# Layer norms from shifted sums taken beside the last projection, first and last recurrence pair beside projections, rotation without TensorE

## The chip, the cores and the metric

One NeuronCore of one Trainium2 chip runs the kernel. The metric is the device time of one execution in microseconds, the median of several runs. Engines are called by their profile names: PE (TensorE), DVE (VectorE), ACT (ScalarE), POOL (GpSimd), SP (SyncE, which here only issues DMAs).

## The reference

`reference()` takes x of 512 positions x 2048 channels through two blocks. Cut to what matters here:

```
first_block:  h = rms_norm(x)*(1+scale)+shift;  proj = h @ w_in
              q = rope(rms_norm(q)), k = rope(rms_norm(k)), 8 heads: sparse attention
              8 heads: chunked HGRN2 recurrence;  x += gate * (concat @ w_out)
second_block: y = even_layer(x)      # stick-breaking attention, pooling, @ w_out
              x = layer_norm(ALPHA * x + y, ln_g[0], ln_b[0])
              y = odd_layer(x)       # mixes x with its predecessor, @ w1, @ a1,
                                     # r,k,v,g = mixed @ w_r, w_k, w_v, w_g
                                     # wkv7 recurrence over 32 heads, group norm, @ w_o
              x = layer_norm(ALPHA * x + y, ln_g[1], ln_b[1])
layer_norm:   mean = mean(x); var = mean((x - mean)**2); (x - mean)*rsqrt(var+eps)*g + b
rope:         (t1*cos - t2*sin, t2*cos + t1*sin) of the two halves of a head's channels
```

All of it is float32.

## The kernel before

Activations lie transposed: 16 tiles `X[kt]` of 128 channels x 512 positions. Every projection is cut into groups `G` of 512 output channels; a group is four slots `k`, a slot covers four input tiles. SP loads a slot's weights (1 MB) into `RAW[k % 2]`, ACT copies them as rounded floats into `WH` (L308), DVE writes the remainder into `WL` (L313), and PE does three matmuls of 128x512 for each of the 16 pairs of input and output tile (`pe_slot`, L288 to L290): 192 matmuls a group. The result lies in four PSUM banks, `PJ` or `AB`. The input side is split in the same way when the source changes ("refill" number `e`: `act_refill` writes `XH`, L383, `dve_refill` writes `XL`, L388, tile by tile). Before the first slot of a refilled group PE waits for four `XL` tiles.

`act_group` and `dve_group` give the order on ACT and DVE: in step k >= 1 the split of the slot after next, then the side work `steps(k)`; after the last slot the evacuation `evac()`, side work 3 and 4, and the split of slot 1 of the next group. So side work placed in step k delays the next split on that engine.

The stages in order: modulation rows (`ada`), index keys and queries, selection of keys by DVE, eight attention heads (`att_*`; head h-1 is computed as side work of the projection group of head h), eight HGRN heads, the output projection `G_OUT1`, eight stick-breaking heads, four pooling groups, `G_OUT2` with its layer norm (`ln_pe`, `ln_act`, `ln_dve`, l = 0), the narrow group `G_LORA`, sixteen groups `G_RW` (r, k, v, g; stored to `rkvg_scratch` by POOL), the recurrence, `G_OUT3`, and the second layer norm.

In attention, the rotation of q and k is: PE multiplies both with a matrix that swaps the halves (L428), DVE forms AB * SIN and wk * COS and adds them (L490 to L493).

A layer norm here follows the evacuation of the last group: PE sums over the channels with a matrix of 1/2048 (L914), DVE subtracts the mean from 16 tiles (L936), ACT squares (L924), PE sums the squares (L917), ACT takes the root (L926), DVE the reciprocal (L939) and 16 products (L942), ACT scales and shifts (L929). After the first norm ACT and DVE then split the 16 tiles for the group `G_LORA`, whose slot 2 is split by DVE only after its first mixing step (L1123).

The recurrence is written as a loop over t from -3 (unrolled) in which each engine's list `wv_pe`, `wv_act`, `wv_dve`, `wv_sp`, `wv_pool` treats four pairs of heads at different stages. A pair's triangular block goes from SBUF to HBM (`sp_blocks_out`, L1241) and back (L1245), POOL solves it (L1291, L1294), the result goes out and back (L1259, L1264), DVE transposes it (L1649). Before the loop SP waits for all stores of r, k, v, g and for three memsets of POOL, writes zeros (L1790) and loads pairs 0 and 1. After it, ACT waits for all 16 pairs before the first split and refill of `G_OUT3`.

## Time and profile before

| what | us |
|---|---|
| median of 3 runs (3834.82 to 3844.33) | 3836.2 |
| the profiled execution | 3836.17 |
| its span in the trace | 3834.5 |
| PE busy in the span | 3507.2 (91%) |
| DVE busy | 1774.2 (46%) |
| ACT busy | 1399.7 (37%) |
| POOL busy | 364.6 (10%) |
| granted PE clock, mean | 0.955 of full |

Busy time of PE is the time in which any matmul was in flight. Times inside the trace count from the span's start. A matmul of a projection starts 0.23 us after the one before it although its own row says 0.4 us, because matmuls are pipelined. A "chain" is followed back from the last instruction of a window to what released each step, so it shows which engine set the end there.

### The profile page before, as it was taken

The numbers are of one execution on the slowest core, as the hardware profiler recorded it, in microseconds if no ns is written. First come the engines' busy times: TensorE is split into PE (matmuls) and PEld (weight loads), VectorE is DVE, ScalarE is ACT, GpSimd is POOL, SyncE is SP. The second block draws the span as 40 slices with busy tenths as digits, with TensorE's granted clock in tenths as the row PEclk, the third lists the DMA queues.
The fourth block names the chain that finished last, engine by engine and source line by source line (L and its number), as shares of the span: only waits on it lengthen the run. The fifth ranks groups of instructions, "written<-read, shape, count | busy, mean of one in ns | idle before, by whom it ended". The sixth has DMA issues, their size and how long they took to land.

```text
span 3834.5 us, 51471 instructions
## 1 busy us (share of the span) xinstructions
PE 3507.2 (91%) x21068; PEld 2729.5 (71%) x21068; DVE 1774.2 (46%) x2242; ACT 1399.7 (37%) x1625; POOL 364.6 (10%) x718
## 2 busy tenths in 40 slices
PE   8998899999998798999999987999999958888797
PEld 1476677777877587777777774888888846666584
DVE  3547645556666423333332336342424226776434
ACT  1322233243343212333322215241414137887323
POOL 0001121222121000000000000000000013333000
PEclk9998999999999799999999998999999979999798
DMA  8422122322222142222222222333333323332321
GB/s 303 174 77 74 66 96 90 98 99 87 90 94 85 61 161 103 77 77 77 88 90 85 99 89 81 119 118 114 120 120 131 109 68 76 73 78 59 107 96 66
DMA packets 178951, 381.37 MB, mean 99 GB/s; under 512 B 111728, under 2 KB 117104, under 8 KB 145008
## 3 DMA queue, kind: packets, MB, share of 16 engines
q1 hardware_dynamic: 164352, 326.73, 25.3%
q0 software_dynamic: 14448, 52.50, 4.1%
q8 instruction: 110, 1.80, 0.2%
q14 instruction: 41, 0.34, 0.0%
HBM read 342.49 MB, written 35.13 MB: 98 GB/s over the span
## 4 chain that ended last, share of the span: by engine, by line
PE 76%; DVE 9%; ACT 5%; DMA 3%; issue 3%; POOLq 2%; SPq 1%; DVEq 1%; ACTq 1%; POOL 0%
PE PJ L288 15%; PE PJ L290 15%; PE PJ L289 15%; PE AB L288 6%; PE AB L289 6%; PE AB L290 6%; PE AB L229 2%; DVE WL L313 1%; POOLq L1293 1%; POOLq L1290 1%; PE AB L917 1%; DVE XL L388 1%; DVE WK L853 1%; DMA WS<-solved_scratch 1%; DMA X<-blocks_scratch 1%
## 5 line engine op out<-in xcount | busy, mean ns | idle before, releaser
L288 PE MATMUL PJ<-XH,WH 128*128 128x512 f32 x2848 | 1138.6, 400 | 100.0 <-DVE XL L388 58.1
L290 PE MATMUL PJ<-XH,WL 128*128 128x512 f32 x2848 | 1119.1, 393 | 0.0
L289 PE MATMUL PJ<-XL,WH 128*128 128x512 f32 x2848 | 1118.9, 393 | 0.0
L313 DVE TENSOR_TENSOR WL<-RAW,WH 128x2048 fp32r<-128x2048 f32 (+2 forms) x240 | 552.9, 2305 | 729.7 <-ACT WH L308 724.7
L308 ACT ACTIVATE WH<-RAW 128x2048 fp32r<-128x2048 f32 (+2 forms) x240 | 453.0, 1889 | 917.1 <-PE PJ L290 633.8
L288 PEld LDWEIGHTS PJ<-XH,WH 128*128 128x128 f32 x2848 | 542.0, 190 | 224.7 <-issue 81.5
L289 PEld LDWEIGHTS PJ<-XL,WH 128*128 128x128 f32 x2848 | 542.1, 190 | 115.6 <-issue 5.0
L290 PEld LDWEIGHTS PJ<-XH,WL 128*128 128x128 f32 x2848 | 540.8, 190 | 115.1
L288 PE MATMUL AB<-XH,WH 128*128 128x512 f32 (+1 forms) x960 | 375.5, 391 | 25.3 <-DVE XL L388 22.4
L289 PE MATMUL AB<-XL,WH 128*128 128x512 f32 (+1 forms) x960 | 375.3, 391 | 0.0
L290 PE MATMUL AB<-XH,WL 128*128 128x512 f32 (+1 forms) x960 | 375.1, 391 | 0.0
L288 PEld LDWEIGHTS AB<-XH,WH 128*128 128x128 f32 (+1 forms) x960 | 179.3, 187 | 66.4 <-issue 26.6
L290 PEld LDWEIGHTS AB<-XH,WL 128*128 128x128 f32 (+1 forms) x960 | 179.3, 187 | 40.0
L289 PEld LDWEIGHTS AB<-XL,WH 128*128 128x128 f32 (+1 forms) x960 | 179.3, 187 | 39.7
L229 PE MATMUL AB<-WK,SMALL 128*1 128x512 f32 x192 | 90.8, 619 | 16.9 <-DMA WK<-ada 16.9
L1291 POOL TENSOR_TENSOR X<-X 128x30 f32<-128x30 f32 (+10 forms) x240 | 73.3, 305 | 218.0 <-DMA X<-blocks_scratch 185.6
L400 ACT ACTIVATE WK<-PJ 128x1024 f32<-128x1024 f32 (+1 forms) x23 | 23.1, 1005 | 178.8 <-PE PJ L290 178.8
L406 DVE COPY WK<-PJ 128x1024 f32<-128x1024 f32 (+1 forms) x31 | 37.4, 1207 | 101.7 <-PE PJ L290 101.6
L1856 POOL DMA_DIRECT2D rkvg_scratch<-WK x16 | 12.0, 753 | 741.7 <-DVE WK L1149 741.7
L540 POOL TENSOR_TENSOR TBL<-GATE,SMALL 128x512 f32<-128x512 f32 x16 | 16.8, 1048 | 660.0 <-PE AB L555 657.2
L1294 POOL TENSOR_TENSOR X<-X 128x30 f32<-128x30 f32 (+10 forms) x240 | 72.9, 304 | 34.7 <-issue 1.2
L229 PEld LDWEIGHTS AB<-WK,SMALL 128*1 128x1 f32 x192 | 15.1, 85 | 82.3 <-issue 82.2
(374 smaller groups left out, 3907.4 us busy)
## 6 DMA issues: line engine op xcount, KB each, us to landing
RAW<-w SPq DMA_DIRECT2D x232, 1024.0 KB, 4.8
WK<-ada SPq DMA_DIRECT2D x32, 1024.0 KB, 4.9
GATE<-gate POOLq DMA_DIRECT2D x64, 256.0 KB, 2.9
rkvg_scratch<-WK POOLq DMA_DIRECT2D x16, 1024.0 KB, 4.8
x_scratch<-X POOLq DMA_DIRECT2D x8, 1024.0 KB, 5.7
X<-rkvg_scratch SPq DMA_DIRECT2D x32, 256.0 KB, 3.4
RAW<-rkvg_scratch SPq DMA_DIRECT2D x32, 256.0 KB, 3.6
X<-xT SPq DMA_DIRECT2D x4, 1024.0 KB, 15.6
```

Of the source, the lines that this page charges most:

```text
L229: m = nc.tensor.matmul(AB[0:1, 2 + b, :], SILU[:, SKT * k + j:SKT * k + j + 1], WK[:, at:at + SEQ], start=k == 0 and j == 0, stop=False)
L288: nc.tensor.matmul(bank[0:width, n, :], hi, xh, start=first, stop=False)
L289: nc.tensor.matmul(bank[0:width, n, :], hi, xl, start=False, stop=False)
L290: m = nc.tensor.matmul(bank[0:width, n, :], lo, xh, start=False, stop=last)
L308: nc.scalar.activation(WH[k % 2][:, :, 0:w], narrow(RAW[k % 2], w), ACT.Copy).then_inc(wh_ready, 1)
L313: nc.vector.tensor_tensor(WL[k % 2][:, :, 0:w], narrow(RAW[k % 2], w), WH[k % 2][:, :, 0:w].bitcast(F32), ALU.subtract).then_inc(wl_ready, 1)
L388: nc.vector.tensor_tensor(tile(XL, kt), src(kt), tile(XH, kt).bitcast(F32), ALU.subtract).then_inc(xl_ready, 1)
L853: nc.vector.reciprocal(wk(12), wk(12))
L917: nc.tensor.matmul(AB[:, 1, :], mat("mean2048"), SQR[kt % 2], start=kt == 0, stop=kt == KT - 1).then_inc(s("ln_used"), 1)
L1290: nc.gpsimd.drain()
L1291: P_TT(SCRATCH[:, 0:c, 0:w], n[:, j:j + 1, j + 1:].to_broadcast([P, c, w]), SOLVED[:, 0:c, j:j + 1].to_broadcast([P, c, w]), ALU.mult)
L1294: m = P_TT(SOLVED[:, 0:c, j + 1:], SOLVED[:, 0:c, j + 1:], SCRATCH[:, 0:c, 0:w], ALU.subtract)
```

## The change

Six things are done.

- **Refilled groups.** `pe_slot` takes the input tile as its outer loop in a refilled group and waits for one `XL` tile at a time.
- **Rotation.** PE no longer swaps the halves. DVE reads the other half of the partitions directly: four instructions on 128x1024 or 64x1024 elements, all from SBUF.
- **Layer norms.** DVE has always summed the tiles as they were evacuated; now the sum of the first 12 tiles gives a provisional mean `SHIFT` after slot 0 of the last group. In steps 1 and 2 of that group DVE subtracts it from 12 tiles, ACT squares them, and POOL adds up the squares (11 additions). Tiles 12 to 15 are finished one by one in slot 3, between PE's output tiles, and PE sums them and their squares by eight small matmuls, among the group's own and behind them. The rest of the mean (`OFF`) is then subtracted by DVE (4 tiles) and POOL (12 tiles), the variance corrected by its square, and DVE's products begin. For l = 0 ACT writes `XH` directly from the product, and DVE's `XL` is interleaved with the products.
- **First pair.** Loads, decay, key norm and the first factor of pair 0 are computed as side work of the last `G_RW` group; SP loads both first pairs there, and POOL fetches the row of resets long before.
- **Last pair.** ACT and DVE split slot 0 and the finished tiles of `G_OUT3` while pair 15 is still worked on; PE waits only for what it needs.
- **Buffers.** Several buffers of the recurrence move so that the above do not overwrite each other (`ws`, `kept`, `T_*`); the lists of the loop keep their order.

```diff
+    wait(pe, wl_ready, g + 1)
+    order = [(n, j) for n in range(tiles) for j in range(SKT)]
     if refill is not None:
-        wait(pe, xl_ready, KT * refill + SKT * (k + 1))
...
+        order.sort(key=lambda nj: nj[1])
+    for n, j in order:
+        kt = SKT * k + j
+        if refill is not None and n == 0:
...
+        if between is not None and j == SKT - 1 and n < tiles - 1:
+            m.then_inc(s("ln_tile"), 1)
+            between(n)
...
-        wait(pe, s("at_qn"), h + 1)
-        for j in range(2):
-            m = nc.tensor.matmul(AB[:, j, :], mat("swap128"), wk(j), start=True, stop=True)
-        m.then_inc(s("at_swapped"), 1)
+        return
...
-        wait(dve, s("at_swapped"), h + 1)
-        for j in range(2):
-            nc.vector.tensor_tensor(wk(6 + j), AB[:, j, :], SIN, ALU.mult)
-            nc.vector.tensor_tensor(wk(j), wk(j), COS, ALU.mult)
+        low, high = slice(0, P // 2), slice(P // 2, P)
+        qk = lambda i, part: wk(i, 2)[part].rearrange("p (j n) -> p j n", j=2)
+        pair = lambda t, part: t[part].unsqueeze(1).to_broadcast([part.stop - part.start, 2, SEQ])
+        nc.vector.scalar_tensor_tensor(qk(6, low), qk(0, high), -1.0, pair(SIN, high), ALU.mult, ALU.mult)
+        nc.vector.tensor_tensor(qk(6, high), qk(0, low), pair(SIN, low), ALU.mult)
+        dve.drain()
+        nc.vector.tensor_tensor(qk(0, slice(0, P)), qk(0, slice(0, P)), pair(COS, slice(0, P)), ALU.mult)
         dve.drain()
         nc.vector.tensor_tensor(wk(4, 2), wk(0, 2), wk(6, 2), ALU.add).then_inc(s("at_roped"), 1)
...
-SUM, RSTD = TBL[:, 0:SEQ], TBL[:, SEQ:2 * SEQ]
+SUM, SHIFT = TBL[:, 0:SEQ], TBL[:, SEQ:2 * SEQ]
 SQR = [TBL[:, (2 + i) * SEQ:(3 + i) * SEQ] for i in range(2)]
+SUMQ, OFF = TBL[:, 4 * SEQ:5 * SEQ], TBL[:, 5 * SEQ:6 * SEQ]
+RSTD = SUM
+EARLY = KT - 4
+OFF_DVE = 4
+POOL_STEPS = EARLY - 1 + KT - OFF_DVE
...
+            if n == EARLY - 4:
+                dve.drain().then_inc(s("ln_sum"), 1)
...
+def ln_mean_pe(pe, l, k):
+    if k == 0:
+        pe.wait_ge(s("ln_sum"), l + 1)
+        nc.tensor.matmul(PJ[:, 0, :], mat("mean2048"), SUM, start=True, stop=True).then_inc(s("ln_mean"), 1)
+def ln_off_pe(pe, l, j):
+    pe.wait_ge(s("ln_xc"), KT * l + EARLY + j + 1)
+    m = nc.tensor.matmul(PJ[:, 1, :], mat("mean2048"), tile(X, EARLY + j), start=j == 0, stop=j == 3)
+    if j == 3:
+        m.then_inc(s("ln_mean"), 1)
+def ln_ms_pe(pe, l, j):
+    pe.wait_ge(s("ln_sq"), KT * l + EARLY + j + 1)
+    nc.tensor.matmul(PJ[:, 2, :], mat("mean2048"), SQR[j % 2], start=False, stop=j == 3
+                     ).then_inc(s("ln_ms"), 1)
+def ln_between_pe(pe, l, n):
+    if n == 1:
+        pe.wait_ge(s("ln_added"), POOL_STEPS * l + EARLY - 1)
+        nc.tensor.matmul(PJ[:, 2, :], mat("mean2048"), SUMQ, start=True, stop=False)
+        ln_off_pe(pe, l, 0)
+    elif n == 2:
+        ln_ms_pe(pe, l, 0)
+        ln_off_pe(pe, l, 1)
+        ln_ms_pe(pe, l, 1)
+def ln_last_pe(pe, l):
+    ln_off_pe(pe, l, 2)
+    ln_ms_pe(pe, l, 2)
+    ln_off_pe(pe, l, 3)
+    ln_ms_pe(pe, l, 3)
+def ln_square_act(act, l, kt):
+    act.wait_ge(s("ln_xc"), KT * l + kt + 1)
+    if kt == 0:
+        nc.scalar.activation(SUMQ, tile(X, 0), ACT.Square).then_inc(s("ln_sq"), 1)
+        return
+    if kt < EARLY + 2:
+        wait(act, s("ln_added"), POOL_STEPS * l + kt - 2)
+    else:
+        act.wait_ge(s("ln_ms"), 4 * l + kt - EARLY - 1)
+    nc.scalar.activation(SQR[kt % 2], tile(X, kt), ACT.Square).then_inc(s("ln_sq"), 1)
+def ln_steps_act(act, l, k):
+    if k == 1:
+        act.wait_ge(s("ln_mean"), 2 * l + 1)
+        nc.scalar.activation(SHIFT, PJ[:, 0, :], ACT.Copy, scale=D / (P * EARLY)).then_inc(s("ln_shift"), 1)
+    if k in (1, 2):
+        for kt in range(EARLY // 2 * (k - 1), EARLY // 2 * k):
+            ln_square_act(act, l, kt)
+def ln_last_act(act, l):
+    for kt in range(EARLY, KT):
+        ln_square_act(act, l, kt)
+    act.wait_ge(s("ln_mean"), 2 * l + 2)
+    nc.scalar.activation(OFF, PJ[:, 1, :], ACT.Copy).then_inc(s("ln_shift"), 1)
+    nc.scalar.activation(SHIFT, PJ[:, 1, :], ACT.Square).then_inc(evac_a, 1)
...
+        if l == 0:
+            act.wait_ge(src_ready, KT * 4 + kt + 1)
+            nc.scalar.activation(tile(XH, kt), tile(X, kt), ACT.Identity, scale=col("ln_g", kt),
+                                 bias=col("ln_b", kt)).then_inc(xh_ready, 1)
+        else:
+            act.wait_ge(s("ln_scaled"), kt + 1)
...
+def ln_steps_dve(dve, l, k):
+    if k not in (1, 2):
+        return
+    if k == 1:
+        dve.wait_ge(s("ln_shift"), 2 * l + 1)
+    for kt in range(EARLY // 2 * (k - 1), EARLY // 2 * k):
+        nc.vector.tensor_tensor(tile(X, kt), tile(X, kt), SHIFT, ALU.subtract).then_inc(s("ln_xc"), 1)
+    if k == 2:
+        if l == 0:
+            dve.wait_ge(s("res_in"), 16 * 8)
+        for j in range(4):
+            x = tile(X, EARLY + j)
+            nc.vector.scalar_tensor_tensor(x, x if l else wk(j), ALPHA, SHIFT, ALU.mult, ALU.subtract)
+        dve.drain()
+def ln_last_dve(dve, l, G):
+    for j in range(4):
+        if j < 3:
+            dve.wait_ge(s("ln_tile"), 3 * l + j + 1)
+        else:
+            dve.wait_ge(slot_done, SLOTS * (G + 1))
+        x = tile(X, EARLY + j)
+        nc.vector.tensor_tensor(x, x, AB[:, j, :], ALU.add).then_inc(s("ln_xc"), 1)
+    dve.drain().then_inc(evac_d, 1)
...
+    dve.wait_ge(s("ln_shift"), 2 * l + 2)
+    nc.vector.tensor_tensor(tile(X, 0), tile(X, 0), OFF, ALU.subtract).then_inc(s("res_added"), 1)
+    dve.wait_ge(s("ln_ms"), 4 * l + 4)
+    dve.wait_ge(evac_a, (G_OUT3 if l else G_OUT2) + 4)
+    nc.vector.tensor_tensor(RSTD, PJ[:, 2, :], SHIFT, ALU.subtract).then_inc(s("ln_sd"), 1)
+    for kt in range(1, OFF_DVE):
+        nc.vector.tensor_tensor(tile(X, kt), tile(X, kt), OFF, ALU.subtract)
+    dve.wait_ge(s("ln_sd"), 2 * l + 2)
     nc.vector.reciprocal(RSTD, RSTD)
     dve.drain()
     for kt in range(KT):
-        nc.vector.tensor_tensor(tile(X, kt), tile(X, kt), RSTD, ALU.mult).then_inc(s("ln_scaled"), 1)
+        if kt >= OFF_DVE:
+            dve.wait_ge(s("ln_added"), POOL_STEPS * l + EARLY + kt - OFF_DVE)
+        m = nc.vector.tensor_tensor(tile(X, kt), tile(X, kt), RSTD, ALU.mult)
+        if l:
+            m.then_inc(s("ln_scaled"), 1)
+            continue
+        m.then_inc(src_ready, 1)
+        if kt > 1:
+            ln_split_dve(dve, kt - 2)
+    if l == 0:
+        for kt in range(KT - 2, KT):
+            ln_split_dve(dve, kt)
...
+def ln_pool(pool, l):
+    for kt in range(1, EARLY):
+        pool.wait_ge(s("ln_sq"), KT * l + kt + 1)
+        if kt > 1:
+            pool.drain()
+        nc.gpsimd.tensor_tensor(SUMQ, SUMQ, SQR[kt % 2], ALU.add).then_inc(s("ln_added"), 1)
+    pool.wait_ge(s("ln_shift"), 2 * l + 2)
+    for kt in range(OFF_DVE, KT):
+        nc.gpsimd.tensor_tensor(tile(X, kt), tile(X, kt), OFF, ALU.subtract).then_inc(s("ln_added"), 1)
...
     pe.wait_ge(wv("osq"), t + 1)
     nc.tensor.matmul(bank(4), mat("mean64"), ws(T_O2), start=True, stop=True).then_inc(wv("ovar"), 1)
+def first_pe(pe, k):
+    if k == 0:
+        pe.wait_ge(evac_a, G_OUT3 - 1)
+        pe.wait_ge(evac_d, G_OUT3 - 1)
+        pe_lora(pe, 0)
...
+def first_act(act, k):
+    if k == 1:
+        act_key_square(act, 0)
+        act_key(act, 0)
+        act_gate(act, 0)
+    elif k == 2:
+        act_lora(act, 0)
+        act_decay(act, 0)
+        act_key_norm(act, 0)
+        act_rate(act, 0)
+        act_growth(act, 0)
+        act_chunk_decay(act, 0)
...
 def dve_gate(dve, q):
     dve.wait_ge(wv("sg"), q + 1)
     V(ws(kept(q) + T_GS), src(q, T_G), ws(T_SG), ALU.mult).then_inc(wv("gs"), 1)
+def first_dve(dve, k):
+    if k == 2:
+        dve_sums(dve, 0)
...
+    sp.wait_ge(s("rk_stored"), 16 * 13)
+    sp.wait_ge(s("res_stored"), 128)
+    sp.wait_ge(slot_done, SLOTS * (G_RW + 13))
+    sp_load(sp, 0)
+    sp_load_lora(sp, 0)
+    sp.wait_ge(wl_ready, SLOTS * G_OUT3 - 1)
+    sp_load(sp, 1)
+    sp_load_lora(sp, 1)
     sp.wait_ge(s("rk_stored"), 256)
...
+    def pe_out_ln(G0, refill, l):
+        for g in range(4):
+            pe_group(pe, G0 + g, refill=refill if g == 0 else None, bank=(PJ, AB)[g % 2], ago=1,
+                     steps=(lambda k: ln_mean_pe(pe, l, k)) if g == 3 else None,
...
+    def last_refill_act(tiles):
+        for kt in tiles:
+            act.wait_ge(wv("done"), kt + 1)
+            nc.scalar.activation(tile(XH, kt), wk(kt), ACT.Copy).then_inc(xh_ready, 1)
...
-    act.wait_ge(wv("done"), PAIRS)
-    for k in range(2):
-        act_split(act, G_OUT3, k)
-    act_refill(act, 9, lambda kt: wk(kt), G_OUT3)
...
+    act_level(act, PAIRS - 1, 1)
+    act_pq(act, PAIRS - 1)
+    act_oa(act, PAIRS - 1)
+    act_out_norm(act, PAIRS - 2)
+    act_split(act, G_OUT3, 0)
+    act.wait_ge(wv("done"), PAIRS - 2)
+    last_refill_act(range(10))
+    act.wait_ge(wv("done"), PAIRS - 1)
+    last_refill_act(range(10, PAIRS - 1))
+    act_out_square(act, PAIRS - 1)
+    act_out_norm(act, PAIRS - 1)
+    act_split(act, G_OUT3, 1)
+    last_refill_act(range(PAIRS - 1, PAIRS))
...
     nc.vector.tensor_scalar(OMKA, COL[:, COLS["k_a"]:COLS["k_a"] + KT], -1.0, 1.0, ALU.mult, ALU.add)
     dve.drain()
     dve.wait_ge(s("reset_in"), 16)
-    for t in range(-3, PAIRS + 1):
+    for g in range(4):
+        dve_group(dve, G_RW + 12 + g, rw_dve(dve, 12 + g, (PJ, AB)[g % 2]), last=g == 3,
+                  steps=(lambda k: first_dve(dve, k)) if g == 3 else None)
+    for t in range(-3, PAIRS):
         wv_dve(dve, t)
+    dve_split(dve, G_OUT3, 0)
+    dve.drain()
+    dve_refill(dve, 9, lambda kt: wk(kt), range(4))
     nc.vector.memset(SUM, 0.0)
...
+    wv_dve(dve, PAIRS)
+    dve.drain()
+    dve_refill(dve, 9, lambda kt: wk(kt), range(4, 8))
+    dve_split(dve, G_OUT3, 1)
+    dve_refill(dve, 9, lambda kt: wk(kt), range(8, KT))
```

## Rows read from the trace of the kernel before

**Rows 1.** The page: chain that ended last by engine; costliest groups (busy, mean ns)
```profile
PE 76%; DVE 9%; ACT 5%; DMA 3%; issue 3%; POOLq 2%; SPq 1%; DVEq 1%; ACTq 1%; POOL 0%
...
L313 DVE TENSOR_TENSOR WL<-RAW,WH 128x2048 fp32r<-128x2048 f32 (+2 forms) x240 | 552.9, 2305 | 729.7 <-ACT WH L308 724.7
L308 ACT ACTIVATE WH<-RAW 128x2048 fp32r<-128x2048 f32 (+2 forms) x240 | 453.0, 1889 | 917.1 <-PE PJ L290 633.8
```

**Rows 2.** Stretches: from:to, length, PE, PEld, DVE, ACT, POOL busy, PEclk, DMA share, GB/s
```profile
3090.00:3214.00 124.00, 74.08 (x1152) 54.81 (x1152) 53.22 (x85) 72.94 (x102) 34.79 (x99) 0.78 0.33 84
3214.00:3550.00 336.00, 294.69 (x5934) 228.53 (x5934) 239.65 (x408) 277.34 (x388) 116.97 (x388) 0.97 0.32 70
```

**Rows 3.** PE's waits over the span: total us, times, longest
```profile
PE PJ L288 <- DVE XL L388: 58.1, 6, 15.8
```

**Rows 4.** Chain in an attention head (start, us, what): the swap of halves
```profile
471.92 1.72 PE AB L428 x4
```

**Rows 5.** DVE in time order: split of slot 2 in a head; XL of a refill
```profile
470.14 2.29 DVE L313 TENSOR_TENSOR WL<-RAW,WH 128x2048 fp32r<-128x2048 f32 x1
...
1475.44 9.72 DVE L388 TENSOR_TENSOR XL<-X,XH 128x512 fp32r<-128x512 f32 x16 [0.74 <-ACT XH L383]
```

**Rows 6.** DVE in time order, both norms: evacuations, last XL tile, LORA's slot 2
```profile
2290.00 1.28 DVE L896 SCALAR_TENSOR_TENSOR X<-WK,AB 128x512 f32<-128x512 f32 x2 [7.52 <-PE AB L290]
...
2360.51 0.69 DVE L388 TENSOR_TENSOR XL<-X,XH 128x512 fp32r<-128x512 f32 x1 [0.74 <-ACT XH L383]
...
2370.02 1.76 DVE L313 TENSOR_TENSOR WL<-RAW,WH 128x1536 fp32r<-128x1536 f32 x1 [1.55 <-ACT WH L308]
...
3788.34 1.28 DVE L896 SCALAR_TENSOR_TENSOR X<-X,AB 128x512 f32<-128x512 f32 x2 [17.46 <-PE AB L290]
```

**Rows 7.** ACT in time order: XH of the last refill; the second norm's last step
```profile
3606.85 8.41 ACT L383 ACTIVATE XH<-WK 128x512 fp32r<-128x512 f32 x16
...
3820.68 11.39 ACT L929 ACTIVATE X<-X,COL 128x512 f32<-128x512 f32 x16 [4.19 <-DVE X L942]
```

**Rows 8.** DVE in time order beside POOL's additions; a reciprocal beside them
```profile
904.98 1.77 DVE L751 TENSOR_TENSOR WK<-WK 128x512 f32<-128x512 f32 x1
...
1237.12 3.35 DVE L853 RECIPROCAL WK<-WK 128x512 f32<-128x512 f32 x1 [4.29 <-ACT WK L819]
```

**Rows 9.** POOL in time order in the same two places
```profile
904.60 1.61 POOL L544 TENSOR_TENSOR TBL<-TBL,GATE 128x512 f32<-128x512 f32 x1 [1.44 <-issue]
...
1239.25 1.05 POOL L542 TENSOR_TENSOR GATE<-GATE,SMALL 128x512 f32<-128x512 f32 x1
```

**Rows 10.** Chain from the last G_RW group on: first transpose and two later (start, us)
```profile
3094.46 4.72 DMA rkvg_scratch<-WK
...
3102.74 0.67 SPq L1790
...
3129.53 0.62 SPq L1241
...
3157.81 0.72 DVE WS L1649
...
3374.26 0.71 DVE WS L1649
...
3427.55 0.71 DVE WS L1649
```

**Rows 11.** Chain through the last pairs to G_OUT3 (start, us)
```profile
3553.81 1.81 PE PJ L1394 x32
...
3577.97 3.70 PE PJ L1394 x32
...
3590.07 0.64 ACT X L1563
...
3596.05 2.09 PE AB L1451 x2
...
3609.67 2.42 DVE XL L388 x4
```

More of the change, by code:

```diff
@@ new lines, in pe_slot @@
+                order.sort(key=lambda nj: nj[1])
+            for n, j in order:
+                kt = SKT * k + j
+                if refill is not None and n == 0:
+                    wait(pe, xl_ready, KT * refill + kt + 1)
+                hi = WH[k % 2][:, j, n * width:(n + 1) * width]
+                lo = WL[k % 2][:, j, n * width:(n + 1) * width]
+                xh, xl = tile(XH, kt), tile(XL, kt)
+                first, last = k == 0 and j == 0, k == SLOTS - 1 and j == SKT - 1
+                nc.tensor.matmul(bank[0:width, n, :], hi, xh, start=first, stop=False)
+                nc.tensor.matmul(bank[0:width, n, :], hi, xl, start=False, stop=False)
+                m = nc.tensor.matmul(bank[0:width, n, :], lo, xh, start=False, stop=last)
+                if between is not None and j == SKT - 1 and n < tiles - 1:
+                    m.then_inc(s("ln_tile"), 1)
+                    between(n)
@@ L291, in pe_slot, with pe_group @@
             m.then_inc(slot_done, 1)
-        def pe_group(pe, G, steps=None, refill=None, tiles=4, bank=None, ago=0, width=P):
+        def pe_group(pe, G, steps=None, refill=None, tiles=4, bank=None, ago=0, width=P, between=None):
             wait(pe, evac_a, G - ago)
@@ L348, in act_group @@
                     steps(k)
-            wait(act, slot_done, SLOTS * (G + 1))
+            if not by_tile:
+                wait(act, slot_done, SLOTS * (G + 1))
             evac()
@@ L357, in act_group, with dve_group @@
                 pre()
[L359 removed]
+        def dve_group(dve, G, evac, steps=None, pre=None, last=False, split=dve_split, next_split=dve_split, by_tile=False):
             for k in range(SLOTS):
@@ L366, in dve_group @@
                     steps(k)
-            wait(dve, slot_done, SLOTS * (G + 1))
+            if not by_tile:
+                wait(dve, slot_done, SLOTS * (G + 1))
             evac()
@@ L905, in f @@
                         dve.drain()
+                    if n == EARLY - 4:
+                        dve.drain().then_inc(s("ln_sum"), 1)
             return f
-        for name in ("sum", "mean", "xc", "sq", "used", "sd", "scaled", "out"):
+        for name in ("sum", "mean", "shift", "tile", "xc", "sq", "added", "ms", "sd", "scaled", "out"):
             s("ln_" + name)
-        def ln_pe(pe, l):
-            wait(pe, s("ln_sum"), l + 1)
-            nc.tensor.matmul(AB[:, 0, :], mat("mean2048"), SUM, start=True, stop=True).then_inc(s("ln_mean"), 1)
-            for kt in range(KT):
-                wait(pe, s("ln_sq"), KT * l + kt + 1)
-                nc.tensor.matmul(AB[:, 1, :], mat("mean2048"), SQR[kt % 2], start=kt == 0,
-                                 stop=kt == KT - 1).then_inc(s("ln_used"), 1)
```

177 lines of the change are left out of this document (79 added, 98 removed).

## The prediction

> **What bounds the kernel now.** I read the page first: its chain that ended last is 76% PE, 9% DVE, 5% ACT [rows 1]. So time is saved only where PE runs something that can go, or stands still. Then the stretches: in the first 124 us from the end of the r, k, v, g groups on PE is busy for 74.1 us at a granted clock of 0.78, in the middle of the pair loop for 294.7 of 336 us at 0.97 [rows 2]. Then PE's waits: 58.1 us in six waits before the first matmul of a slot, for `XL` [rows 3]. The chain and each engine in order of time give the rest [rows 4 to 11]. Outside the gaps a projection costs 0.227 us a matmul: a slot of 48 is 10.9 us, a group 43.6 us; an attention head costs that and its own matmuls. Only the gaps and the float32 matmuls of the side work can give.
>
> The profiled execution (3836.17, span 3834.5, so 1.7 us around it) is the median of the runs (3836.2); I sum against 3836.2.
>
> **Refills.** PE waited for four `XL` tiles, now for one. `XL` takes 9.72/16 = 0.61 us a tile [rows 5], against 12 matmuls = 2.7 us that PE does with it, so PE never runs dry afterwards: 3 x 0.6 = 1.8 us each at the even layer's first group and at `G_OUT2`. At `G_OUT1` slot 0's tiles are made ahead of DVE's other work, slot 1's are waited for again: 2.1 + 1.8 = 3.9. The group of k and w gains nothing, since slot 2's `WL` is next behind it. Sum 7.5 (bounds 3 and 10). The other order of matmuls costs nothing: same count, same weights loaded.
>
> **Rotation.** The swap is four entries, 1.72 us of PE in a head [rows 4]: a float32 matmul of 512 columns costs 0.86. It goes, in eight heads. But DVE's slot 2 split ends at 472.43 [rows 5], and PE, now 1.72 ahead, would reach that slot 0.5 before: 1.2 is left. Head 0 is set by DVE's selection and gains nothing: 7 x 1.2 = 8.2. DVE's rotation is two instructions on half the partitions, one product, one sum, each 1024 elements long, 2 x 0.6 = 1.23: 5 us, about what six did before; done by 477.5, and PE wants it at the end of the slot, 482.8: 5 us of cover. Reading 64 partitions and writing the other 64, and the second input repeated by a zero stride, are in no row. Bounds: if they run at the normal rate, 8.2, and 12 if the split is early enough; at half rate they take 5 more, and the gain falls to nothing.
>
> **Layer norm 0.** Reference points: the last evacuation starts at 2290.0, and `G_LORA`'s slot 2 is split at 2371.8, 81.8 us later [rows 6]; PE can't pass slot 2 before that in either kernel. Six small matmuls fall inside the group (mean, sum of squares, four for tiles 12 and 13): 6 x 0.86 = 5.2 us. What then follows PE's end: tile 15, its mean and square, `OFF`: 3.3; the root at 10.4 (`WL` of `G_LORA`'s slot 1 lies ahead); reciprocal 3.35 [rows 8] to 13.8; 16 times a product and an `XL` tile, the latter 0.69 [rows 6] and the pair 1.42, to 37.3, the mixing step and split of slot 2, 11.3, to 48.6. With 5.2 that is 53.8: a gain of 28.0, if DVE and POOL run side by side.
>
> They may not. An operation of 0.6 us on DVE ran for 1.77, from 904.98 [rows 8], while POOL's addition ended at 906.21 [rows 9]: it ended 0.54 after it. A reciprocal, one input, took its 3.35 [rows 8] with a POOL operation inside it [rows 9]. So two-input operations take turns: a POOL one 1.25 (nearest: 1.05 [rows 9]; 1.23 is left of the 1.61 from 904.98 on), then a DVE one 0.6. I take this, since every step of the norm is such an operation on both engines.
>
> The Trainium skill ("SBUF — State Buffer", on who interferes with whom) says the same of the port pair: an exclusive lock, taken by turns, between GpSimd and a VectorE instruction with two SBUF inputs, while one with a single SBUF input goes on. The two places above agree; what it leaves open is who wins how often in a row.
>
> By turns: in steps 1 to 3 of the last group DVE's 6 subtractions and 4 products (6.0), 6 of POOL's additions (7.5), `G_LORA`'s first split with its scaling (5.4 by turns; such a split alone is 1.76 [rows 6]) and a tile's addition (0.6), from 2273.3 (the end of step 1's split, 16.7 before the reference point), put the shifted tile 12 at 2293.1. PE wants it after two banks of slot 3 (2290.0 - 10.9, + 0.9 for the mean, + 5.5, + 0.9 for the sum of squares: 2286.3): 6.8 us of waiting, and the group ends 12.1 later than before. Behind it the reciprocal runs from 15.3 to 18.7 after PE's end, POOL's twelve subtractions end at 24.9 (they had to take turns with nothing from 15.3 on), products and `XL` end at 44.5, slot 2 at 55.8. 12.1 + 55.8 = 67.9: a gain of 13.9, less 1 for matmuls at the lower clock: **13.0**.
>
> **Layer norm 1.** From the last evacuation's start, 3788.34 [rows 6], to the end of the span it is 46.2 us; ACT's last 16 operations take 11.39, 0.71 each, and end at 3832.07 [rows 7], the output DMA 2.4 later. New, side by side: 5.2, reciprocal 6.5 to 9.9, 16 outputs 0.71 apart and the product ahead, to 22.1, DMA 24.5: 29.7, a gain of 16.5. By turns: 6.7 (1.5 of waiting; no `G_LORA` split is in DVE's way here), reciprocal to 13.05, POOL's last subtraction at 24.9, the products behind it to 30.9, ACT 32.6, DMA 35.0: 41.7, a gain of **4.5**.
>
> **First pair.** Before: the last store of r, k, v, g lands at 3099.18, SP then writes zeros (0.67 an issue), loads two pairs, and pair 0's block goes out at 3129.53 [rows 10]. Its load, decay, key norm and first factor now lie beside the last group. SP still waits for the last store and writes four zeros: 3099.2 + 2.7 = 3102.0, and the block can go: 27.5 earlier. POOL's memsets (three, already behind it) and the 28.3 us to DVE's transpose at 3157.81 [rows 10] stay, and pair 1's block, some 22 behind pair 0's, stays ahead of it. PE pays 2.6 for the small matmuls, which now lie in a busy stretch: **24.9**. ACT's and DVE's side work is 14.5 us of a group of 46.2, and ends 2 before it by the lists. In the loop ACT is busy for 277.3/336 = 83%, DVE 71%, PE 88% [rows 2]; a pair takes 53.3 (3427.55 - 3374.26 [rows 10]); each list only lost its first round. Bounds 18 and 28. The loop's period stays: the chain there is POOL's and DMA's latency around the block.
>
> **Last pair.** Before: ACT's last split begins at 3590.7, behind the root that starts at 3590.07, `XH` is 8.41 for 16 tiles, and PE starts at the end of `XL`'s first four, 3609.67 + 2.42 = 3612.1 [rows 11, 7]. Now ACT splits slot 0 (1.89 [rows 1]) from 3590.7 to 3592.6, 15 `XH` tiles 0.526 apart end at 3600.5, then the square 0.6; the variance's matmuls, which began at 3596.05 and took 2.09 [rows 11], come behind it: 3603.3, and PE goes on with `G_OUT3`, its first `XL` done at 3600.1. 8.9, less 0.7 for a later load of the next weights: **8.2** (bounds 3 and 10). This makes pair 15's own chain later than before, which is covered by the three slots that need not wait for its tile.
>
> Moved buffers, memsets and waits within lists are equal in number and cost nothing.
>
> **Sum.** 7.5 + 8.2 + 13.0 + 4.5 + 24.9 + 8.2 = 66.3: 3836.2 - 66.3 = 3769.9, I say **3770**. Side by side the norms give 26.7 more (15 and 12 to the turns' 13.0 and 4.5): 3743.
>
> **Rivals.** (A) DVE and POOL do not get in each other's way in the norms, since DVE queues its operations back to back and POOL fills the rest: 3743 to 3749. For it: a row of either engine beside the other is rare in this trace. Against: 904.98 above. (B) POOL wins several times in a row, and DVE's side work for pair 0 outlasts its group: the norms give nearly nothing (17 less) and the first pair no less than 18: 3776 to 3786. For it: POOL always has its next operation ready. (C, slower) The clock. Now 32 matmuls of the inverse take 1.81, and 3.70 where PE had stood still before them [rows 11]: half rate, 1.2 instead of 2.4 GHz. The loop stays at 0.97 [rows 2] because PE's side streams lie close together. If the other places of the buffers or the lost first round shift PE's lists so that four such sets run at half rate in every pair, that is 4 x 1.89 = 7.6 us a pair, 121 in 16: 3890. It decides from 66/16 = 4.1 us a pair on, some two sets. Against: lists and waits of the loop are in the same order, and PE is busy for 88%. (D) The change doesn't do what it says, because another wait (the store, the lora split) lies behind each: 3836 at most, within 0.3%.
>
> **How the numbers follow.** Forecast (3758 to 3776, turns as costed) 0.58; A 0.22; B 0.13; C 0.04; D 0.02; the last 0.01 lies beyond A. The predicted time is the forecast's. 3744 to 3786 holds the forecast, B and nearly all of A; its ends come from A's sum and from the low bounds of rotation and pairs. 0.3%, 11.5 us, is about what measurement can tell from no change here. Faster by more: all but C and D, 0.94; within: D, 0.02; slower: C, 0.04.
>
> **What would show it.** An attention head's period falls by 1.2 us, with no wait of PE for the rotated q; at twice the price of DVE's half-partition operations PE waits in front of slot 3. In norm 0: slot 2 of `G_LORA` is split 56 us after the last group's end (A: 49; B: over 65), that group is 12 longer than the one before it (A: 5), and DVE operations beside POOL's subtractions last 1.9 instead of 0.6 (A: all 0.6). In norm 1: from the last group's end to the end of the span 35 instead of 46. Pair 0's block leaves within 3 us of the last store's landing. The pair's period stays 53.3 (C: 57 or more). `G_OUT3` starts 9 us earlier after the last inverse. Wrong would make it: a store or weight load that is late where the gap was, a longer pair period, or a last group that waits for shifted tiles by more than 7 us.

## The result and the profile after

The changed kernel takes 3780.4 us in the median of four runs (3775.1 to 3787.2), the kernel before 3837.4 beside it (3834.8 to 3844.3). The ratio is 0.9845, interval 0.983 to 0.986: 57 us less. I had forecast 66 less than 3836.2, 3770, range 3744 to 3786.

The profiled execution of the changed kernel took 3787.2, with a span of 3785.5, so it is the slowest of its four. Between the two traces lie 49.0 us, not 57; a second trace of the same kernel has a span of 3784.3. What follows is told from traces, each against its own time.

The page of the changed kernel: its busy times and the engines' shares of the chain that ended last (before: [rows 1]).

```profile
PE 3477.1 (92%) x21008; PEld 2721.9 (72%) x21008; DVE 1818.0 (48%) x2236; ACT 1402.5 (37%) x1627; POOL 434.7 (11%) x764
...
PE 71%; DVE 12%; ACT 5%; DMA 4%; issue 3%; POOLq 3%; SPq 1%; DVEq 1%; ACTq 1%; POOL 0%
```

POOL is busy for 70 us more, DVE's share of the chain rose from 9% to 12%: work came off PE, and part of it lies on the path at DVE. To see where the time went I took the start of DVE's split of slot 2 in each of the 60 groups in both traces, and in the pairs' loop DVE's transpose. The differences, in us gained:

| part | forecast | first trace | second trace | others |
|---|---|---|---|---|
| rotation | 8.2 | 6.0 | 6.3 | 3.3 to 6.3 |
| refills (`G_OUT1`, even layer, `G_OUT2`) | 7.5 | 4.6 | 4.9 | 4.7 to 7.5 |
| layer norm 0 with its group | 13.0 | 14.3 | 14.3 | 13.1 to 14.3 |
| first pair, to the first transpose | 24.9 | 21.4 | 21.6 | 17.7 to 19.7 |
| loop, first to last transpose | 0 | -4.8 | -7.9 | -9.8 to 3.7 |
| last pair, to `G_OUT3`'s second group | 8.2 | 1.2 | 3.9 | 2.1 to 3.6 |
| layer norm 1 with its group | 4.5 | 7.1 | 7.2 | 7.1 to 7.2 |
| start of the kernel | 0 | -0.8 | -0.1 | -1.0 to 0.5 |
| sum | 66.3 | 49.0 | 50.2 | |

The last column is the range over the traces of the experiments below, each counted only in the parts that its edit leaves alone. It tells how much a part moves from trace to trace though its code is the same. Only the norms stand firm to about 1 us. The kernel before moves as well: its second trace is 2.8 us later over the part of the refills, and the version with moved buffers gains 1.7 in the part of the rotation. So a difference of 2 or 3 us between two single traces shows little by itself outside the norms; what counts there is a wait that is seen to come or go.

**Layer norm 0.** DVE in order of time in the changed kernel (start, us for all of the row, line and tiles, count), then POOL, then PE's waits from 2235 to 2352. These answer to [rows 6], [rows 8] and [rows 9].

```profile
2251.80 4.79 DVE L1003 TENSOR_TENSOR X<-X,TBL 128x512 f32<-128x512 f32 x6
...
2264.75 6.98 DVE L1003 TENSOR_TENSOR X<-X,TBL 128x512 f32<-128x512 f32 x6
2271.66 5.76 DVE L1009 SCALAR_TENSOR_TENSOR X<-WK,TBL 128x512 f32<-128x512 f32 x4
...
2281.10 1.76 DVE L318 TENSOR_TENSOR WL<-RAW,WH 128x1536 fp32r<-128x1536 f32 x1 [1.55 <-ACT WH L313]
2282.78 1.28 DVE L1019 TENSOR_TENSOR X<-X,AB 128x512 f32<-128x512 f32 x2
```

```profile
2258.47 1.29 POOL L1056 TENSOR_TENSOR TBL<-TBL 128x512 f32<-128x512 f32 x1 [0.17 <-issue]
...
2269.64 1.55 POOL L1056 TENSOR_TENSOR TBL<-TBL 128x512 f32<-128x512 f32 x1 [0.16 <-issue]
```

```profile
PE AB L290 <- DVE XL L395: 19.9, 1, 19.9
PE AB L290 <- DVE WL L318: 6.5, 1, 6.5
PE PJ L933 <- DVE X L1019: 6.1, 1, 6.1
PE PJ L945 <- POOL TBL L1056: 0.7, 1, 0.7
```

Sixteen operations of DVE on 128x512 with both inputs in SBUF took 9.72 us without POOL, 0.61 each [rows 5], so six cost 3.7; in step 2, with POOL beside them from the third on, they took 6.98, and the four products 5.76 instead of 2.5. A POOL addition is 1.29 alone and 1.55 with DVE beside it. That is the taking of turns: from there on one operation of POOL and one of DVE end alternately, a turn of each in 1.70 us, 0.2 less than 1.29 and 0.6. It delays `G_LORA`'s split, and the split delays tile 12, for which PE waits 6.1 us (forecast 6.8). The wait of 6.5 is the one before `G_LORA`'s slot 2.

**Layer norm 1.** DVE, then POOL, to the end of the span at 3785.5.

```profile
3752.82 0.69 DVE L1019 TENSOR_TENSOR X<-X,AB 128x512 f32<-128x512 f32 x1 [4.63 <-PE AB L292]
...
3757.24 4.49 DVE L1029 TENSOR_TENSOR X<-X,TBL 128x512 f32<-128x512 f32 x3
3761.65 3.34 DVE L1031 RECIPROCAL TBL<-TBL 128x512 f32<-128x512 f32 x1
3765.07 16.23 DVE L1036 TENSOR_TENSOR X<-X,TBL 128x512 f32<-128x512 f32 x16
```

```profile
3756.07 19.26 POOL L1059 TENSOR_TENSOR X<-X,TBL 128x512 f32<-128x512 f32 x12 [14.44 <-ACT TBL L981]
```

POOL's twelve subtractions take 19.26, 1.6 each, and DVE's products beside them 1.67 each until POOL is through; the reciprocal, one input, is unstretched in the middle of it. From the last evacuation (3752.82) to the end it is 32.7 us, forecast 35.0.

### The profile page after: what moved, and what is told of

Same layout as the page of the kernel before. It is cut to its first block, busy times and chain, and to the rows that moved or that the text cites. A ratio compares the mean times of both kernels' runs of the same rounds, so it can differ in the third digit from the quotient of the medians.

```text
span 3785.5 us, 51414 instructions
## 1 busy us (share of the span) xinstructions
PE 3477.1 (92%) x21008; PEld 2721.9 (72%) x21008; DVE 1818.0 (48%) x2236; ACT 1402.5 (37%) x1627; POOL 434.7 (11%) x764
## 4 chain that ended last, share of the span: by engine, by line
PE 71%; DVE 12%; ACT 5%; DMA 4%; issue 3%; POOLq 3%; SPq 1%; DVEq 1%; ACTq 1%; POOL 0%
PE PJ L290 15%; PE PJ L291 15%; PE PJ L292 15%; PE AB L290 5%; PE AB L291 5%; PE AB L292 5%; PE AB L229 2%; DVE WL L318 2%; DVE WK L486 1%; POOLq L1412 1%; POOLq L1409 1%; DMA X<-blocks_scratch 1%; DVE WK L860 1%; DMA WS<-solved_scratch 1%; DMA blocks_scratch<-WS 1%
## 5 line engine op out<-in xcount | busy, mean ns | idle before, releaser
L547 POOL TENSOR_TENSOR TBL<-GATE,SMALL 128x512 f32<-128x512 f32 x16 | 16.5, 1031 | 654.9 <-PE AB L562 651.8
```

## Experiments

### Whose turn it is

Theory: both of DVE's inputs in SBUF is what makes it take turns with POOL. The edit puts one of them into PSUM, in seven lines of which three are shown; besides, one wait of DVE moves ahead of its first subtraction, which then starts 3.8 us instead of 3.2 after the last evacuation of the second norm's group.

```diff
-            nc.vector.tensor_tensor(tile(X, kt), tile(X, kt), SHIFT, ALU.subtract).then_inc(s("ln_xc"), 1)
+            nc.vector.tensor_tensor(tile(X, kt), tile(X, kt), PJ[:, 3, :], ALU.subtract).then_inc(s("ln_xc"), 1)
...
-            nc.vector.reciprocal(RSTD, RSTD)
+            nc.vector.reciprocal(PJ[:, 3, :], RSTD)
...
-                m = nc.vector.tensor_tensor(tile(X, kt), tile(X, kt), RSTD, ALU.mult)
+                m = nc.vector.tensor_tensor(tile(X, kt), tile(X, kt), PJ[:, 3, :], ALU.mult)
```

> In the two norms one operand of each DVE operation that runs beside POOL (the provisional mean, the rest of the mean, the reciprocal root) is read from PSUM instead of SBUF; counts and sizes are the same, POOL does what it did. Theory (DVE and POOL take turns because both of DVE's inputs lie in SBUF): DVE's operations beside POOL last 0.6 to 0.7 instead of 1.6 to 1.7, POOL's 1.3 instead of 1.5 to 1.6, PE's wait for the shifted tile 12 falls from 6.1 to under 3 in the first norm; the second norm's tail from the last evacuation to the end of the span falls from 32.7 to about 25, the first norm gives about 8 to 12: together 16 to 20 us, some 0.995 of the changed kernel's time. Rival (the two are slow beside one another whatever the operands, or POOL alone sets the pace at 1.6 a tile): all stays within 3 us.

Measured: 3768.9 us in the median (3768.7 to 3775.7), ratio to the kernel before 0.9821 (0.980 to 0.984). DVE and POOL in both norms of this kernel, then PE's waits from 2238 to 2340:

```profile
2263.88 3.66 DVE L1003 TENSOR_TENSOR X<-X,PJ 128x512 f32<-128x512 f32 x6
2267.47 2.47 DVE L1009 SCALAR_TENSOR_TENSOR X<-WK,PJ 128x512 f32<-128x512 f32 x4
2270.01 3.02 DVE L329 TENSOR_TENSOR RAW<-RAW,COL 128x384 f32<-128x384 f32 x2
...
3749.29 0.69 DVE L1019 TENSOR_TENSOR X<-X,AB 128x512 f32<-128x512 f32 x1 [4.63 <-PE AB L292]
...
3759.47 9.65 DVE L1036 TENSOR_TENSOR X<-X,PJ 128x512 f32<-128x512 f32 x16
```

```profile
3752.54 14.77 POOL L1059 TENSOR_TENSOR X<-X,TBL 128x512 f32<-128x512 f32 x12 [15.08 <-ACT TBL L981]
```

```profile
PE AB L290 <- DVE XL L395: 14.4, 1, 14.4
PE AB L290 <- DVE WL L318: 5.9, 1, 5.9
PE PJ L933 <- DVE X L1019: 3.0, 1, 3.0
```

The same six operations take 3.66 instead of 6.98, the sixteen products 9.65 instead of 16.23, POOL's twelve 14.77 instead of 19.26. What has all its inputs in SBUF is still stretched, `G_LORA`'s scaling for one: 3.02 for the two operations that take 1.03 with POOL idle. The tail is 24.7 instead of 32.7, the first norm gains 23.0 instead of 14.3, the second 16.2 instead of 7.1. Together that is 17.8 us in the traces, of the 16 to 20 expected; the rival falls. The Trainium skill ("SBUF — State Buffer", Who interferes with whom) has only the pair of ports that DVE's second SBUF input shares with GpSimd as a cause of contention, an exclusive lock; the trace agrees in which operations are stretched and which are not.

The whole time fell by less, 9 us by the ratios and 11.5 between the two traces: the first pair and the loop, which this edit does not touch, gave 7.6 less in this trace. The wait for `WL` before `G_LORA`'s slot 2 stays (5.9, in the changed kernel 6.5), and behind it 12 of PE's matmuls run at the lower rate instead of 8, so that one group further on the first norm's gain is 22.1.

The counter-test leaves the operands in SBUF and takes POOL away from the second half of the norms (`OFF_DVE = 4` becomes `16`: DVE subtracts the rest of the mean from all 16 tiles).

> The changed kernel, but all 16 subtractions of the rest of the mean are DVE's; POOL does none, and DVE's operands stay in SBUF. Theory (a POOL subtraction costs DVE 1.1 us of turn and saves it 0.6): second norm's tail from the last evacuation to the end 31.4 instead of 32.7, DVE's products 0.6 each, first norm within 1 us; in all 0 to 3 us less although POOL's help is gone. Rival (POOL's twelve subtractions do help): both tails 4 to 6 us longer.

Measured: 3777.6 (3771.0 to 3789.2), ratio 0.9829 (0.981 to 0.985), which can't be told from the changed kernel. In the trace the sixteen products:

```profile
3769.54 3.34 DVE L1031 RECIPROCAL TBL<-TBL 128x512 f32<-128x512 f32 x1
3772.96 9.72 DVE L1036 TENSOR_TENSOR X<-X,TBL 128x512 f32<-128x512 f32 x16
```

The second norm's tail is 31.4 (3787.5 - 3756.1), as expected to the tenth; the first norm gained 11.6, where traces with POOL's help have 13.1 to 14.3, more than the 1 us allowed. So POOL's help in the form that the change gives it is worth -1.3 us in one norm and 1.5 to 2.7 in the other: about nothing.

### The split of G_LORA ahead of tile 12

The edit starts the split behind tile 13's addition and square; two further lines, not shown, take it out of its old place.

```diff
     for kt in range(EARLY, KT):
         ln_square_act(act, l, kt)
+        if l == 0 and kt == EARLY + 1:
+            act_lora_split(act, G_LORA, 0)
...
+        if l == 0 and j == 1:
+            dve_lora_split(dve, G_LORA, 0)
```

> The changed kernel, but in the last group of G_OUT2 the first split of G_LORA (DVE's scaling, ACT's WH, DVE's WL, 5.4 us on DVE) stands behind the additions of tiles 12 and 13 instead of ahead of them. Theory (PE's wait of 6.1 us for the shifted tile 12 came from that split, delayed by turns with POOL): the wait falls below 1, the tiles 14 and 15 wait for nothing new, the group is 5 to 7 us shorter and so is the time. Rival (the split, moved, delays tile 14's addition or the first products of the norm by as much): under 2 us.

Measured: 3773.0 (3770.9 to 3773.6), ratio 0.9828 (0.981 to 0.985). In the trace the wait is 0.8 instead of 6.1 and the norm gains 21.0 instead of 14.3: 6.7 us. The theory holds. DVE's ten operations in step 2 are stretched as before, so the turns alone would have cost PE little; they cost 6 us because a split that nobody needed yet was queued on DVE behind them and ahead of what PE waited for.

### The rotation

PE's waits from 440 to 500, one head, in the changed kernel; DVE there (the four operations of 1.22 and 1.23 are the rotation):

```profile
PE AB L452 <- ACT WK L472: 2.1, 2, 1.1
PE PJ L290 <- DVE WL L318: 0.8, 1, 0.8
```

```profile
469.64 2.29 DVE L318 TENSOR_TENSOR WL<-RAW,WH 128x2048 fp32r<-128x2048 f32 x1 [0.17 <-issue]
471.96 1.22 DVE L495 SCALAR_TENSOR_TENSOR WK<-WK,TBL 64x1024 f32<-64x1024 f32 x1
473.20 1.22 DVE L496 TENSOR_TENSOR WK<-WK,TBL 64x1024 f32<-64x1024 f32 x1
474.49 1.22 DVE L498 TENSOR_TENSOR WK<-WK,TBL 128x1024 f32<-128x1024 f32 x1
475.79 1.23 DVE L500 TENSOR_TENSOR WK<-WK 128x1024 f32<-128x1024 f32 x1
```

The heads' period fell by 0.6, not 1.2, 4.4 us over seven heads. The rest of the table's 6.0 lies ahead of these heads and behind them; ahead of them traces of kernels that are alike there differ by more than 2 us. Half the partitions, moved to the other half, cost the normal rate, as taken. The split of slot 2 ends 28.1 us after a fixed point of the head, PE's score matmuls (471.93 - 443.83), instead of 27.8 (472.43 [rows 5] - 444.60), since the change puts a drain ahead of it, and PE waits 0.8 and not 0.5. The edit moves two products and that drain behind the split:

```diff
                 nc.vector.reciprocal(wk(6, 2), wk(6, 2))
                 dve.drain()
+            elif k == 1:
                 nc.vector.scalar_tensor_tensor(wk(0), wk(0), col("qg"), wk(6), ALU.mult, ALU.mult)
                 nc.vector.scalar_tensor_tensor(wk(1), wk(1), col("kg"), wk(7), ALU.mult, ALU.mult)
                 dve.drain()
-            elif k == 1:
```

> In the attention heads the two products that finish q and k (0.75 us each, and the drain behind them) stand behind DVE's split of slot 2 instead of ahead of it; nothing else changes. Theory (of the 1.72 us of PE that the rotation frees, 1.1 is lost again because slot 2's WL now ends after PE is there: a wait of 0.8 in the trace, and some restart): no wait of PE for WL there, head period 53.5 instead of 54.6, 7 x 1.1 = 7 to 8 us less. Rival (the loss is the clock or the longer DVE rotation, which ends nearer to its use): period stays 54.6 or PE waits in front of slot 3 instead.

Measured: 3772.3 (3769.1 to 3781.6), ratio 0.9828 (0.981 to 0.985). The wait is gone from the head; the period is 1.8 shorter than before (expected 1.7), 12.0 us over seven heads; the whole part of the table gives 14.4 instead of 6.0. The 1.72 us that PE no longer works in a head becomes time only when DVE's split is ready by the time PE gets there.

### First pair, loop, last pair

The chain of the changed kernel, from the last evacuation to the first transpose, beside [rows 10]:

```profile
3073.84 1.24 DVE WK L1266
...
3076.89 5.52 POOLq L2020
...
3082.49 0.63 SPq L1945
...
3085.22 0.64 SPq L1360
...
3112.40 0.72 DVE WS L1789
```

From the evacuation's end to the block's issue it is 10.1 us instead of 36.1, to the transpose 37.3 instead of 64.3: 27.0 gained, forecast 27.5. POOL's clearing (L2020), which ends at 3082.4, and the store, whose last packet ends at 3081.9, are over about together. But the last group is 5.7 longer, not 2.6: PE waited 2.8 us in step 0 for pair 0's table, which SP may load only behind the group's own weights.

The price can be higher. PE's two small matmuls behind that wait, in the changed kernel and in the one of the first experiment:

```profile
3038.28 1.10 PE L1423 MATMUL PJ<-TBL 96*128 96x512 f32 x2 [2.77 <-DMA TBL<-lora]
```

```profile
3030.28 2.05 PE L1423 MATMUL PJ<-TBL 96*128 96x512 f32 x2 [3.16 <-DMA TBL<-lora]
```

In the second PE came back at the lower of its two rates (granted clock 0.71 from 3026.8 to 3038.5, against 1.00 at the same place of the first), and the next six matmuls of the projection ran at 0.43 instead of 0.23. So it was in six of the eight traces without the edit below; the group is 8.2 to 9.3 us longer there, and that is why the table has 17.7 to 19.7 beside 21.4 and 21.6.

The edit takes PE's small matmuls to step 1 (`if k == 0` and `elif k == 1` become one `if k == 1`).

> The changed kernel, but in the last group of r, k, v, g PE does pair 0's two small matmuls of the decay in step 1 instead of step 0. Theory (the table of pair 0 is loaded only after that group's last weight load is issued, and PE waited 2.8 us for it in step 0): that wait goes, ACT gets the result in time for its step 2, the last group is 2.5 to 3 us shorter. Rival (ACT's side work is late then, or the first solve is set by the last store of r, k, v, g and POOL's clearing, not by PE): under 1 us.

Measured: 3771.5 (3767.4 to 3781.1), ratio 0.9831 (0.980 to 0.986). The wait is gone, the group is 2.6 longer as forecast, and the way from the last group's slot 2 to the first transpose gains 24.7 instead of 21.4, or instead of the 17.7 to 21.6 of all eight traces: my forecast of 24.9 was right but for this. The rival, under 1 us, falls.

**The loop.** I took nothing for it. It was 4.8 longer in the first trace, and three further traces were to tell what that is.

> The changed kernel once more, unchanged, for its loop. In the first profile the sixteen transposes of the pairs (DVE WS 128x512, once a pair) lay 27.50 us apart in the mean, in the kernel before 27.18, 4.8 us in all. Theory 1 (chance: the loop's period wanders from run to run): another mean, anywhere from 27.1 to 27.6. Theory 2 (the moved buffers or the missing round cost something): 27.5 again. All else as in the first profile: head period 54.6, slot 2 of G_LORA 14 us earlier within its stage than before, last group to end of span 32.7.

> The kernel before once more, for the same question: theory 1 says a mean distance of the pairs' transposes anywhere from 27.1 to 27.6, theory 2 says 27.2 again.

> The kernel before with nothing but the new places of the recurrence's buffers (two in GATE, one in WK, the others renumbered, the kept ones rotated by one). In two profiles of the kernel before the pairs' transposes lay 27.17 and 27.18 us apart, in four with the change 27.50 to 27.77, 5 to 9 us over fifteen. Theory (the places cost it): 27.5 to 27.8 here, and 5 to 9 us more than the kernel before. Rival (it is the start: pair 0 is further ahead of pair 1 when the loop begins, and PE and its clock settle differently): 27.2 here, the same time as before.

Over fifteen distances the period is 27.71 in the changed kernel once more, 27.17 in the kernel before, and 27.84 in the kernel before with the buffers moved. 27.71 lies above what theory 1 allowed, too; by the last trace the places cost 10 us. But that kernel's median of ten runs is 3840.5 beside 3837.8 for the kernel before in thirteen, ratio 0.9998, interval 0.9985 to 1.0011, at most 4 us, where the theory wanted 5 to 9. The other kernels, whose loop is that of the changed one, show how far the period wanders. The stretch from the first to the fifteenth transpose (from:to, length, busy us of PE, PEld, DVE, ACT, POOL, granted clock, DMA share, GB/s) in the kernel before, then the changed one, the one with moved buffers, and the one with PE's matmuls in step 1:

```profile
3157.81:3539.32 381.51, 333.86 (x6792) 260.28 (x6792) 267.73 (x455) 315.13 (x442) 133.17 (x434) 0.97 0.32 72
```

```profile
3112.40:3500.65 388.25, 338.49 (x6792) 264.08 (x6792) 267.35 (x454) 315.16 (x442) 136.09 (x434) 0.96 0.31 71
```

```profile
3159.66:3551.55 391.89, 342.91 (x6781) 267.67 (x6782) 267.91 (x454) 313.88 (x440) 134.44 (x434) 0.94 0.31 69
```

```profile
3106.43:3484.38 377.95, 333.33 (x6786) 259.48 (x6786) 267.53 (x455) 314.41 (x440) 132.25 (x434) 0.97 0.32 72
```

DVE's and ACT's work is the same in all, POOL's to 4 us; the length goes with PE's clock. Over thirteen traces the mean period of this stretch runs from 27.0 at 0.97 to 28.1 at 0.94, with a correlation of -0.90. So the missing round has no fixed price, since two traces with it lie at 27.0 and 27.2, and the places of the buffers cost at most 4 us; but the stretch differs by up to 16 us between traces, with more of PE's time at the lower of its two rates where it is long. Whether the clock makes the loop slow or a slow loop lets the clock fall isn't shown by these, nor whether the new places make it more frequent: of the eleven traces with them eight lie at 27.7 or above, seven of the ten with the change and the one of the kernel before with moved buffers, and of the two with the old places none. Two are too few to tell. That the kernel before wanders as a whole is on record: its executions took 3830.0 to 3850.9 us, the longest at a granted clock of 0.953, the shortest at 0.958.

**The last pair.** The chain of the changed kernel, beside [rows 11]:

```profile
3551.80 1.89 ACT WH L313
3553.70 7.80 ACT XH L2185 x15
...
3572.12 14.52 DMA RAW<-w
...
3586.66 1.92 ACT WH L313
...
3588.60 2.30 DVE WL L318
...
3590.95 0.79 PE PJ L290
3591.74 0.43 PE PJ L291
```

PE starts `G_OUT3` 21.5 us after the last inverse (3563.15 - 3541.67) instead of 30.7 (3612.34 - 3581.69): 9.2 gained, forecast 8.9. Then it stands for 3.9 us before slot 2, whose weights were issued behind the 4 MB of x and took 14.5 us, and then runs 14 matmuls at 0.43 instead of 0.23, which is 2.8 more. I had written 0.7 for this. Before, PE came to slot 2 so much later that the same load was covered. The edit lets SP issue slot 2's weights ahead of x (`range(2)` and `range(2, SLOTS)` become `range(3)` and `range(3, SLOTS)`).

> The changed kernel, but SP issues the weights of slot 2 of the group G_OUT3 ahead of the 4 MB of x that it reads back, instead of behind them. Theory (in the changed kernel PE stood 3.9 us before slot 2 and ran its next 14 matmuls at half the rate, because the weights landed 14.5 us after their issue, behind x): the weights land some 10 us earlier, no wait of PE before slot 2, 7 us from the last inverse to group G_OUT3 + 1 less. Rival (x, now behind the weights, is what is late: the evacuation of the first group waits for it, or DVE and ACT get to slot 2 no earlier): under 3 us.

Measured: 3775.4 (3774.9 to 3786.9), ratio 0.9835 (0.981 to 0.986). In the trace no wait for `WL` is left there, and from the last transpose to the second group it gains 8.6 against the kernel before instead of 1.2 to 3.9 in the eight traces without the edit. Its median of 5 us below the changed kernel can't be told from nothing; the trace can. x, now issued behind the weights, delays nothing: the next group starts where this one leaves off (42.3 and 42.2 gained at the two).

### The refills

```diff
             if refill is not None:
-                order.sort(key=lambda nj: nj[1])
+                wait(pe, xl_ready, KT * refill + SKT * (k + 1))
             for n, j in order:
...
-                if refill is not None and n == 0:
...
-                    wait(pe, xl_ready, KT * refill + kt + 1)
```

> The changed kernel, but PE waits for four XL tiles again before a slot of a refilled group, and goes through the output tiles first, as in the kernel before. Theory: at G_OUT1 3.0 later, at the even layer's first group 1.1, at G_OUT2 0.4 (these are the differences of before and changed in the traces), at G_LORA nothing (slot 2's split ends the wait), at G_OUT3 nothing or little, since the first four tiles are ready before PE has done the last pair: 4.5 in all. Rival (the order of the matmuls or the one tile matters more than the differences show, as I had forecast): 7.5.

Measured: 3793.9 (3787.5 to 3800.8), ratio 0.9872 (0.985 to 0.989), by the ratios 10 us above the changed kernel. In the trace it is 7.8 later up to the last r, k, v, g group: 3.9 at `G_OUT1`, 1.1, 0.4, 1.0 at `G_LORA`, 1.5 at the first attention groups. From there to the end it loses 5.9 more, most of it in the loop, at a period of 27.84 and a clock of 0.94 in this trace. The 1.5 at the attention groups need not come from the edit: the kernel of the `G_LORA` experiment, unchanged there, is 2.6 later at the same place. What speaks for the size is all traces together: over the part of the refills the nine with the new order gain 4.6 to 7.5, 6.0 in the mean, and the four without it -2.8 to 0, -1.5 in the mean, so 7.5 between them. My term of 7.5 had the right size and partly the wrong places: 1.8 at the even layer and `G_OUT2` were 1.1 and 0.4 in this pair of traces, and I had counted nothing at `G_LORA`, which gives 1.0. Waiting for one tile and the other order of matmuls were not tested apart.

### All edits together

> The changed kernel with all five edits: operands of the norms in PSUM, slot 2's split ahead of the two products of q and k, the weights ahead of x at G_OUT3, pair 0's small matmuls in step 1, the split of G_LORA behind tiles 12 and 13. If each gives what it gave alone, by place in the traces, and the two in the first norm overlap by half (wait of 3.0 left, not 6.1): 8.4 (rotation) + 8.7 + 3 (first norm) + 3 (last group before the recurrence) + 7.3 (G_OUT3) + 9.1 (second norm) = 39 to 40 below the changed kernel, 3741, ratio to the kernel before 0.975. Rival (what one frees the next wait takes: slot 2 of G_LORA, DVE in the heads): 25 to 30, 3750 to 3755.

Measured: 3746.2 us in the median of five runs (3738.8 to 3753.8), the kernel before 3842.1 beside it, ratio 0.9758 (0.974 to 0.978). In the trace (span 3741.4) the heads gain 15.0, the first norm 27.9, the last pair 9.5, the second norm 16.1. PE's waits from 2220 to 2340:

```profile
PE AB L290 <- DVE XL L395: 14.4, 1, 14.4
PE AB L290 <- DVE WL L318: 7.1, 1, 7.1
```

The wait for the shifted tile is gone. 16.1 in the second norm is what I had worked out for engines that run side by side (16.5). In the first norm 27.9 stands beside 28.0 partly by luck: it took the moved split besides the PSUM operands, which alone gave 23.0, and one group further on it is 26.7. The version is 2.4% faster than the kernel before, and by the ratios 0.9%, 33 us, faster than the changed one. That lies between the 39 to 40 expected and the rival's 25 to 30; the wait for `WL` before `G_LORA`'s slot 2 is the one that the rival named, 7.1 now and 6.5 in the changed kernel.

## Why the prediction was right, and where it was not

- **The time**: 3780 lies in the range, 10 above the forecast. It came from terms that were off by up to 7 us and partly cancelled, and the loop, taken as 0, gave anything from -9.8 to 3.7 in single traces: that the sum came so near is in part luck.
- **Turns in the norms**: right in kind, place and size. With one operand in PSUM the second norm is that of rival A, side by side (16.2 of 16.5); the first (23.0 of 28.0) is not, since the split ahead of tile 12 was still in the way. My price of a turn, 1.25 + 0.6 = 1.85, was too high: it is 1.6 to 1.7, less than the two operations' own 1.29 and 0.60 even if POOL's pause of 0.16 falls into DVE's turn; why isn't shown. So POOL was through 2.4 earlier in the second norm, which gained 2.6 more, the first 1.3 more. And of the terms "by turns" one had no turn in it: the split's 5.4 is what it takes beside an idle POOL (2277.49 to 2282.86).
- **Rotation**: the step that failed was that DVE's split ends at 472.43 as before and PE "would reach that slot 0.5 before". I had not counted the drain that the change puts ahead of the split, nor what PE loses when it restarts: 0.6 a head, not 1.2, so 4.4 for 8.2. The bounds held.
- **First pair**: 27.0 of 27.5 on the chain. The cost on PE was 5.7, in other traces up to 9.3, not 2.6: of the moved step I had counted the matmuls but not where the load that they need stands in SP's queue, nor that PE can come back from that wait at half rate.
- **Loop**: "the loop's period stays" was wrong as a term of the sum for a single run; it wanders by 1 us a pair. Rival C named the cause, PE's half rate in the pairs, and priced it as a fixed loss of 121; in small it happens, also in the kernel before with moved buffers (27.84), though in neither of the two traces of the kernel before itself. And I misread [rows 10]: transposes at 3374.26 and 3427.55 are two pairs apart, since the chain passes only through every other one. A pair takes 27, not 53.3. No term of the sum rested on it.
- **Last pair**: 9.2 of 8.9 where PE starts; the term "0.7 for a later load of the next weights" measured 6.7. I had seen that load and not asked what is ahead of it in its queue.
- **Refills**: 4.6 and 4.9 in the two traces against the first of the kernel before, 7.5 in the mean of all traces; forecast 7.5.
